# Eight kept weight units instead of six in a streamed mixture-of-experts block, with an earlier reload and folded norms

## The reference, cut to what matters

```python
def first_block(x, ...):                      # 256 tokens, width 1024
    xn = rms_norm(x, norm1_g); h_in = xn @ w_in
    attn = block_attention(q, k, v)           # 8 query heads, 2 key heads
    lru = (h_f + h_b) * gelu(lru_gate)        # two scans, forward and backward
    x = x + concat(rms_norm(attn, g_a), rms_norm(lru, g_l)) @ w_out
    x = x + moe_ffn(rms_norm(x, norm2_g), ...)   # 32 experts, top 4 of them for a token
    return rms_norm(x, final_g)
def moe_ffn(...):                             # for each expert e and its tokens xb
    g = min(xb @ w_gate[e] + b_gate[e], 7); u = clip(xb @ w_up[e] + b_up[e], -7, 7)
    y = ((u + 1) * g * sigmoid(1.702 * g)) @ w_down[e] + b_down[e]
def second_block(x, mem, ...):                # two layers
    h = h + mixer(rmsnorm(h, norm_mix[l]))    # layer 0: index scores choose keys, attention over them,
                                              #   and pooling; layer 1: a convolution module
    h = h + cross_attn(rmsnorm(h, norm_cross[l]), rmsnorm(mem, norm_mem[l]), ...)
    h = h + swiglu(rmsnorm(h, norm_ffn[l]), ...)
```

## Time and profile before

| | before |
|---|---|
| median of 3 runs | 1995.56 us (1995.07 to 1997.11) |
| the profiled execution's own time | 1995.56 us |
| its span, first to last instruction | 1993.8 us |
| TensorE busy | 1968.9 us (99%) |
| VectorE, ScalarE busy | 849.6 us (43%), 421.1 us (21%) |
| moved from and to memory | 565.20 MB, mean 283 GB/s |
| experts, first multiplication to the end of expert 31 | 189.38 to 1123.6 us |

### The profile page before, as it was taken

How to read it: one execution, slowest core, us unless ns; L and a number is a source line. 1 busy time by engine, 2 the same in 40 slices (tenths; PEclk the granted TensorE clock), 3 DMA queues, 4 the chain that set the end, 5 groups by cost and what they waited for, 6 DMA issues and landing times.

```text
span 1993.8 us, 29849 instructions
## 1 busy us (share of the span) xinstructions
PE 1968.9 (99%) x11290; PEld 1281.3 (64%) x11291; DVE 849.6 (43%) x1801; ACT 421.1 (21%) x827; POOL 22.6 (1%) x56
## 2 busy tenths in 40 slices
PE   9999999999999999999999999999999999999999
PEld 7676333333443344333333587889999886989999
DVE  6644212112122112122121367456766697557774
ACT  4442211112212121122122222231100122331100
POOL 0000000000000000000000020000000000000000
PEclk9999999999999999999999999999999999999999
DMA  9258999999999999999999943424445433334430
GB/s 360 98 209 322 420 422 422 418 421 422 422 391 423 420 422 368 423 422 418 421 422 422 422 173 134 187 97 145 167 168 188 190 128 127 138 116 149 170 133 17
DMA packets 81915, 565.20 MB, mean 283 GB/s; under 512 B 10208, under 2 KB 10880, under 8 KB 14240
## 3 DMA queue, kind: packets, MB, share of 16 engines
q1 hardware_dynamic: 80016, 556.92, 69.8%
q0 software_dynamic: 1808, 6.98, 0.9%
HBM read 559.12 MB, written 4.19 MB: 283 GB/s over the span
## 4 chain that ended last, share of the span: by engine, by line
PE 91%; DMA 7%; ACT 1%; issue 0%; DVE 0%; SPq 0%; ACTq 0%; DVEq 0%
PE bank L669 22%; PE bank L1121 17%; PE bank L620 15%; PE bank L1140 9%; DMA ring<-in_stream 7%; PE bank L1061 3%; PE bank L1043 3%; PE bank L720 3%; PE bank L1164 3%; PE bank L828 3%; PE bank L1106 2%; PE bank L1194 1%; PE bank L1052 1%; PE bank L1418 1%; PE bank L692 1%; PE bank L1347 1%
## 5 line engine op out<-in xcount | busy, mean ns | idle before, releaser
L1121 PE MATMUL bank<-ring,sq 128*64 128x512 f32 x1888 | 416.0, 595 | 9.9 <-DMA ring<-in_stream 9.1
L1121 PEld LDWEIGHTS bank<-ring,sq 128*64 128x64 f32 x1888 | 131.9, 137 | 273.1 <-issue 243.6
L1628 ACT ACTIVATE B<-bank 128x256 f32<-128x256 f32 (+1 forms) x206 | 87.6, 455 | 642.9 <-PE bank L669 335.5
L1140 PE MATMUL bank<-ring,sq 128*64 128x512 f32 x896 | 198.5, 596 | 0.0
L620 PE MATMUL bank<-xn,ring 128*128 128x256 f32 x864 | 191.7, 383 | 0.3
L2595 DVE TENSOR_TENSOR xg<-bank,mbias 128x512 f32<-128x512 f32 x32 | 22.1, 691 | 377.3 <-PE bank L1106 332.7
L620 PEld LDWEIGHTS bank<-xn,ring 128*128 128x128 f32 x864 | 164.9, 192 | 25.4 <-issue 3.6
L669 PE MATMUL bank<-B,ring 128*128 128x128 f32 x1280 | 168.0, 275 | 0.0
L669 PEld LDWEIGHTS bank<-B,ring 128*128 128x128 f32 x1280 | 155.2, 192 | 0.0
L1140 PEld LDWEIGHTS bank<-ring,sq 128*64 128x64 f32 x896 | 61.9, 137 | 116.6 <-issue 116.2
L2575 DVE TENSOR_SCALAR B<-B 128x128 f32<-128x128 f32 x66 | 16.0, 284 | 261.9 <-PE bank L1032 261.9
(11 more groups left out here) (443 smaller groups left out, 2277.3 us busy)
## 6 DMA issues: line engine op xcount, KB each, us to landing
ring<-in_stream SPq DMA_DIRECT2D x513, 1024.0 KB, 14.0
B<-in_stream SPq DMA_DIRECT2D x6, 1024.0 KB, 9.0
mem_kv<-ring POOLq DMA_DIRECT2D x2, 1024.0 KB, 7.1
xT<-in_stream SPq DMA_DIRECT2D x2, 1024.0 KB, 16.1
B<-mem_kv POOLq DMA_DIRECT2D x2, 1024.0 KB, 6.6
xT<-in_x SPq DMA_DIRECT2D x4, 256.0 KB, 5.2
ring<-in_stream SPq DMA_DIRECT2D x4, 256.0 KB, 6.0
ring<-in_mem SPq DMA_DIRECT2D x1, 1024.0 KB, 9.8
```

What stands on the lines that cost most here:

```text
L1121: mm = pe.matmul(PS[4 + kind][NARROW * h:NARROW * (h + 1), :], xs[:, k % 4, NARROW * (k // 4):NARROW * (k // 4 + 1)], weights(e, j, kk, h) ...
L1140: mm = pe.matmul(PS[6][NARROW * h:NARROW * (h + 1), :], hT[0][:, f % 4, NARROW * (f // 4):NARROW * (f // 4 + 1)], weights(e, j, kk, h), st ...
L1628: return act.activation(out_, in_, fn, **kw)
```

## The change

Five edits are made together.

- **Kept units.** Eight units are kept instead of six. Unit 4 goes into the first 2048 columns of `tab`, unit 5 into a new tile `short`, which holds what were `std`, `rinv`, `un`, `rb` and `wr`. The second expert that uses kept units is 27 instead of 24. The reloads begin at turn 9 instead of 13, and come ahead of every second turn (9, 11, ... 23) instead of every one.
- **Early slots.** Ring slots 8 and 11 are loaded as soon as `memn` and the second normalised memory are computed and the 16 early units are used, ahead of the kept units. Slots 10 and 9 are loaded after both spills, as before.
- **Tables.** `tab` is ordered anew. Columns 512 to 2047 (`cos2` to `far`) are no longer loaded at the start. ACT loads them (768 KB) when the last scatter's first bank is done; DVE's index rotary waits for it.
- **Folded norms.** DVE adds the two remaining chunks into one (one more addition of 128 x 256), and `stat` has two multiplications fewer. For the LRU group, DVE adds four chunks to two ahead of its maxima of heads 6 and 7, and `group_sum(1)` has two multiplications fewer.
- **The index weights.** The product for `iw` runs with the weights as the stationary operand, 32 columns wide, in four column groups of the array into bank 6. ACT copies the bank, and two multiplications by a table `fold` add the four groups and transpose. They stand behind the first `iqb` unit.

```diff
-KEPT = (3 * E // 16, 3 * E // 4)
-RELOAD = 13 * E // 32
-KEPT_UNITS = (6, 7, 8, 9, 10, 11)
+KEPT = (3 * E // 16, 27 * E // 32)
+RELOAD = 9 * E // 32
+RELOAD_EVERY = 2
+KEPT_UNITS = (4, 5, 6, 7, 8, 9, 10, 11)
...
-        kept = {8: (reg(0, UNIT),), 9: (reg(UNIT, UNIT),), 7: (reg(2 * UNIT, UNIT),),
+        kept = {4: (tab[:, 0:UNIT],), 5: (short[:, :],), 8: (reg(0, UNIT),), 9: (reg(UNIT, UNIT),), 7: (reg(2 * UNIT, UNIT),),
...
+            for u in range(HELD, EARLY + HELD):
+                sp.wait_ge(S["units_done"], u - HELD + 1)
+                load_first(u)
+            sp.wait_ge(S["memn_ready"], 16)
+            load_first(EARLY + HELD)
+            load_first(EARLY + HELD + 3)
+            sp.wait_ge(S["mixed_ready"], 4)
+            for j in (8, 9, 7, 4):
+                keep(KEPT[0], j)
+            sp.wait_ge(S["o_mm"], 8)
+            sp.wait_ge(S["ksum_mm"], 4)
+            for j in (10, 11):
+                keep(KEPT[0], j)
+            sp.wait_ge(S["kv_spilled"], 32)
+            load_first(EARLY + HELD + 2)
+            load_first(EARLY + HELD + 1)
...
                     keep(KEPT[0], 6)
+                    keep(KEPT[0], 5)
...
             for n, j in enumerate(KEPT_UNITS):
                 keep(KEPT[1], j)
-                for s in range(RING):
-                    load_slot(RELOAD + n, s)
+                for i in range(RELOAD_EVERY):
+                    for s in range(RING):
+                        load_slot(RELOAD + RELOAD_EVERY * n + i, s)
...
                 for b in range(2):
-                    for c in range(2):
-                        mm = pe.matmul(PS[stat_bank(n)][:, b:b + 1], sq[:, c, b * P:(b + 1) * P], tb("ones")[:, 0:1],
-                                       start=(c == 0), stop=(c == 1))
+                    mm = pe.matmul(PS[stat_bank(n)][:, b:b + 1], sq[:, 0, b * P:(b + 1) * P], tb("ones")[:, 0:1],
+                                   start=True, stop=True)
...
-            for b in range(2):
-                for k in range(C):
-                    mm = pe.matmul(PS[5][:, T + 16 * b:T + 16 * b + 16], xn[:, k, b * P:(b + 1) * P],
-                                   ring[:, slot_of(u), C * P + 16 * k:C * P + 16 * k + 16],
-                                   start=(k == 0), stop=(k == C - 1))
+            for k in range(C):
+                r = slice(32 * (k % 4), 32 * (k % 4 + 1))
+                mm = pe.matmul(PS[6][r, 0:T], ring[:, slot_of(u), C * P + 32 * k:C * P + 32 * k + 32], xn[:, k, :],
+                               start=(k < 4), stop=(k >= 4), skip_group_check=True)
             mm.then_inc(S["units_done"], 1)
             stationary(AT["iqb"], two(2), xn)
+            pe.wait_ge(S["iwt_ready"], 1)
+            for b in range(2):
+                pe.matmul(PS[5][:, T + 16 * b:T + 16 * b + 16], iwt[:, b * P:(b + 1) * P], tb("fold"),
+                          start=True, stop=True)
...
+            act.wait_ge(S["moe_mm"], 1)
+            lo, hi = TAT["cos2"], TAT["far"] + 2 * T
+            act.dma_start(tab[:, lo:hi], tables[:, lo:hi]).then_inc(S["tables_loaded"], 16)
...
+                    mark(tt(sq[:, 0:2, :], sq[:, 0:2, :], sq[:, 2 * j:2 * j + 2, :], ALU.add))
+                    if j == 3:
+                        settle()
+                        tt(sq[:, 0, :], sq[:, 0, :], sq[:, 1, :], ALU.add).then_inc(S["ssum_ready"], 1)
...
                 if a == 5:
                     dve.wait_ge(S["units_done"], 2)
                     memory(1)
+                    dve.wait_ge(S["osq_ready"], 1)
+                    tt(sq[:, 4:6, :], sq[:, 4:6, :], sq[:, 6:8, :], ALU.add).then_inc(S["osq_ready"], 1)
```

More of the change, by code:

```diff
@@ L106 @@
     NV += _n
-TABLES = [("cos1", T), ("sin1", T), ("cos2", T), ("sin2", T), ("cos3", T), ("sin3", T), ("rot1", P),
-          ("ident", P), ("ones", P), ("heads", P), ("before", P), ("iota", T),
-          ("far", 2 * T), ("rcount", 64)]
+TABLES = [("cos1", T), ("sin1", T), ("cos2", T), ("sin2", T), ("cos3", T), ("sin3", T), ("far", 2 * T),
+          ("rot1", P), ("ident", P), ("ones", P), ("heads", P), ("before", P), ("iota", T), ("rcount", 64), ("fold", 16)]
 TAT = {}
@@ L206, in build @@
         mbias = sb("mbias", [P, E * 16])
-        wr = sb("wr", [P, C, E])
         br = sb("br", [P, E])
@@ L212, in build @@
         pT = sb("pT", [P, 2, 2, T])
-        std = sb("std", [P, 512])
-        rinv = sb("rinv", [P, 512])
+        short = sb("short", [P, UNIT])
+        std, rinv = short[:, 0:512], short[:, 512:1024]
+        un = short[:, 1024:1536].rearrange("p (a t) -> p a t", a=2)
+        rb = short[:, 1536:1792]
+        wr = short[:, 1792:2048].rearrange("p (c e) -> p c e", c=C)
         small = sb("small", [P, 32])
@@ L313, in build @@
         sc = reg(11728, 2, T)
+        iwt = sc[:, 0, :]
         irot = [reg(a, 2, T) for a in (4640, 5152, 3616, 4128)]
@@ L464, in _ @@
                     load_table("ident", "ones", S["vec_loaded"])
[L465 to L468, removed]
+            for dst, src in ((wr, w_router), (br[:, :], b_router), (mbias[:, :], moe_b)):
+                sp.dma_start(dst, src).then_inc(S["router_loaded"], 16)
+            load_table("before", "fold", S["router_loaded"])
             def keep(e, j):
@@ L549, in _ @@
             pool.wait_ge(S["cv_ready"], 4)
-            pool.dma_start(mem_kv[1], ring[:, HELD + 2, :]).then_inc(S["v_spilled"], 16)
+            pool.dma_start(mem_kv[1], ring[:, HELD + 2, :]).then_inc(S["kv_spilled"], 16)
             pool.wait_ge(S["memn_ready"], 16)
@@ L553, in _ @@
             pool.wait_ge(S["kn_ready"], 2)
-            pool.dma_start(mem_kv[0], ring[:, HELD + 1, :]).then_inc(S["k_spilled"], 16)
+            pool.dma_start(mem_kv[0], ring[:, HELD + 1, :]).then_inc(S["kv_spilled"], 16)
             pool.wait_ge(S["res_ready"], 4)
@@ L856, in group_sum @@
             def group_sum(g, bank):
-                pe.wait_ge(S["osq_ready"], 3 - 2 * g)
-                for c in range(4 if g else 2):
-                    mm = pe.matmul(bank[:, 0:T], tb("ones"), sq[:, 4 * g + c, :], start=(c == 0), stop=(c == (3 if g else 1)))
+                pe.wait_ge(S["osq_ready"], 4 - 2 * g)
+                for c in range(2):
+                    mm = pe.matmul(bank[:, 0:T], tb("ones"), sq[:, 4 * g + c, :], start=(c == 0), stop=(c == 1))
                 mm.then_inc(S["ostat_mm"], 1)
@@ L1961, in _ @@
             f(tv[:, 0, 0:T], PS[5][:, 0:T], ACT.Copy).then_inc(S["iq_ready"], 1)
-            f(iw[:, :, :], PS[5][:, T:T + 32].rearrange("p (a b) -> p a b", a=2), ACT.Copy, scale=1.0 / 32)\
-                .then_inc(S["iw_ready"], 1)
+            f(iwt, PS[6][:, 0:T], ACT.Copy).then_inc(S["iwt_ready"], 1)
             for j in range(2):
@@ L1966, in _ @@
                 f(iqr[:, 4 + 2 * j:6 + 2 * j, :], two(2 + j), ACT.Copy).then_inc(S["iq_ready"], 1)
+            f(iw[:, :, :], PS[5][:, T:T + 32].rearrange("p (a b) -> p a b", a=2), ACT.Copy, scale=1.0 / 32)\
+                .then_inc(S["iw_ready"], 1)
             def relu(h):
@@ L2702, in _ @@
             dve.wait_ge(S["un_ready"], UNSCALED[2] + 2)
+            dve.wait_ge(S["tables_loaded"], 16)
             index_rotary(0, index_pair(0), irot[0], index_pair(0))
@@ L3018, in lay_out_stream @@
     one[:, 0:D] = np.concatenate([ik, ik], 1).reshape(C, P, P).transpose(1, 0, 2).reshape(P, D)
-    one[:, D:D + 16 * C] = w[:, 3072:3088].reshape(C, P, 16).transpose(1, 0, 2).reshape(P, 16 * C)
+    one[:, D:D + 32 * C].reshape(P, C, 32)[:, :, 0:16] = w[:, 3072:3088].reshape(C, P, 16).transpose(1, 0, 2)
     s[AT["pool"]][:, 0:4 * P] = a["pool_w_2"][0].transpose(1, 0, 2).reshape(P, 4 * P)
@@ L3111, in lay_out_tables @@
     put("far", np.where(tok[None, None, :] > q, f(FAR), f(0)).reshape(P, 2 * T))
+    put("fold", (i[:, None] % 32 == np.arange(16)[None, :]).astype(f))
     w = 2 ** np.arange(1, 5)[:, None]
```

36 lines of the change are left out of this document (8 added, 28 removed).

## The result

The changed kernel takes 2002.12 us (median of 7 runs, 2000.3 to 2005.15), the kernel before beside it 1995.79 us (7 runs, 1995.07 to 1998.03). The ratio is 1.0032, 95% interval 1.0023 to 1.0041. So it is slower by 6.3 us, where +2.3 was forecast, and its time lies 0.12 us above the upper end of the range. The profiled execution took 2005.15 us, with a span of 2003.3 us. It is thus 3 us above the median. One execution among those reported further down, of the stream's edits alone, took 8288.52 us and is left out of its time and ratio.

A forecast was written before the change was run, and what follows sets the result against it. TensorE, busy 99%, was taken as the bound, with at most 13.2 us lost to late weights. Terms 4.8 + 1.5 - 2.4 - 2.1 + 0.5 = +2.3 us on 1995.56 gave 1997.9 us, range 1990.5 to 2002.

The forecast's parts named there:

- The stream: Expert stage: the new kept units and reloads make weights later, +4.8 us, bounds -0.6 to some 6.3.
- the ledger: Count of the weight ring's lead over TensorE, limit 11.5 us; gave 16.7 us lost against 11.0, slower by 5.7.
- Run B: Narrow experts 13 to 17: 4.6 us lost to late units before, 1.9 forecast with the change.
- run C: Narrow experts 19 to 31: 6.05 us lost to late units before, 10.2 forecast with the change.
- Run A: Narrow experts 0 to 11: 2.6 us lost to late units before, 4.6 forecast with the change.
- 0.9 us of it stays: Of 5 us given at expert 6, only 0.9 remains: lead at expert 7's unit 7 was 10.6, limit 11.5.
- Rival 1: Faster: early reloads cost nothing, expert lateness goes; 1979.9 us at best, 1986.5 with half; 0.15, including what lies between.
- The LRU group's sum: Ahead of the experts (the front): DVE's addition waits for ACT's squares and delays the output projection, +1.5 us, bounds 0 to 1.8.
- The norms: Four fewer TensorE records save 0.4 us in each of norms 2 to 7, -2.4 us; norms 0 and 1 nothing.
- The index weights: Behind the experts: 16 records in column groups 1.0 us, fold 0.4, instead of 3.5; -2.1 us, bounds 0 to -2.3.
- Rival 2: Slower: DVE or tables take over behind the experts, TensorE's 4.5 us lost, 2002.4 us; 0.27, including the stream's upper bounds.
- The tables: Behind the experts: ACT's transfer issue costs +0.5 us; the load is hidden, as DVE needs it 23 us later.

The follow-up runs named there:

- the swaps apart: Changed kernel with POOL's row swaps of the index queries alternating between two semaphores, each waiting for the swap before the last: 1999.0 us, ratio 1.0013.
- the better reloads: Changed kernel, second kept expert 25 instead of 27, reloads ahead of turns 12 to 19: 1994.46 us, 0.9996; also without the LRU addition: 1992.41 us, 0.9984.
- the three profiles at expert 25: Changed kernel with second kept expert 25, reloads at turns 12 to 19: 1994.46 us; without the LRU addition: 1992.41; also with swaps on two semaphores: 1986.51.

## Why the prediction was wrong, point by point

Three terms of the sum failed. In the profiled execution they were off by 0.7 us (stream and tables' issue, 5.3 forecast and 6.0 measured), 3.3 us (front, 1.5 and 4.8) and 3.7 us (index weights, -2.1 and +1.6). The largest is the gain of the index weights, which did not reach the end.

**The stream: the term was too small.** I took 4.8 between 4.0 and 5.7, and the ledger itself had said 5.7. Late units cost 5.6 us more than before (18.8 against 13.2; the rest of the stage's 6.0 is the tables' issue), and 7 us by the ratio when the stream's edits stood alone. Run B came as forecast, 1.6 for 1.9, run C 10.4 for 10.2. The 1.7 us that run C had lost beyond the ledger before did not return. But they were no accident of one run, as I had supposed: six profiles with the stream of before lost 6.0 to 6.6 us there, and what costs them is open. Run A lost 6.8 for 4.6. So the ledger's 5.7 is near the measured 5.6 by luck: what it misses in run C before and in run A after cancels. In run A the step "0.9 us of it stays" failed. The units behind the full ring, unit 7 and unit 8 of expert 7:

```profile
L501 SPq DMA_DIRECT2D ring<-in_stream x2: 328/328/328, 377.2 to 378.9; - x2
...
DMA to landing us min/median/max: 7.4/8.5/9.7
```

Unit 7 lands at 377.23 + 7.36 = 384.6, where it is needed at 383.51 + 12.2 = 395.7: a lead of 11.1, near the limit of 11.5. But unit 8 lands at 378.94 + 9.68 = 388.6, 4.0 us behind it and not 2.5. In this execution the full ring thus cost transfer time on two units. So the lead that goes on from there is 0.4 + 1.5 us less than the 11.5 of the ledger; 4.6 + 1.9 = 6.5, and 6.8 were lost. It is not so behind every full ring. Behind the second wide expert of the kernel before, the loads issued at 787.04 and 788.76 landed 6.92 and 7.65 us later, 2.5 apart. Of the other four profiles with the changed stream three have unit 8 of expert 7 some 2.8 to 3.6 us behind unit 7, and one 2.5. Experts 9 to 11 lost 6.0 to 6.8 us in all four, so the term was too small in each; why the transfers start again as unevenly as this is open.

Rival 1, faster, is refuted. The reload issued at 404.79 landed at 418.39, 2.49 us behind the load ahead of it, and the next load 2.49 us behind the reload: it took its own length from the stream. The Trainium skill (DMA: Bandwidth & Descriptors, Rules for kernel authors) says of issuing early and waiting late that the fixed setup cost overlaps. I had read it as if the whole transfer were free. This trace does not bear that reading out: between full rings the stream stood at 421 to 422 GB/s, and a transfer moved forward displaced another.

**The LRU group's sum: mechanism right, a second effect missing.** The wait was forecast at 1.5 us; the edit alone moved the projection by 1.4. TensorE's wait there grew from 0.73 to 1.50 us, and one of 0.88 us came ahead of it. In the profiles with the addition the experts start at 190.5, 191.8, 191.9, 191.9 and 194.2, in the nine without it at 188.8 to 191.1, medians 191.9 and 189.4: 2.5 us. The rest goes with the granted clock. Four of the five with it show a stretch at 1.2 GHz there, none of the nine without. The fifth (the swaps apart) had the same wait of 1.50 us and kept its clock, and started 1.1 us late. The prediction had priced the wait and nothing behind it. The upper bound of 1.8 was therefore too low.

**The norms: right.** -2.6 us, forecast -2.4.

**The index weights: the product right, its gain lost.** 16 records took 1.07 us (forecast 1.0) and the fold 0.51 (0.4). The bound "0, if DVE's top-k chain should then be the later one" named the right size and the wrong engine. Not DVE's top-k but POOL's swaps, through DVE and ACT, ended later. The room of 23 us that I had seen for the tables said nothing on the swaps. What I had left out of the price is what the faster engine triggers: the ring's loads come earlier and fall onto the swaps. Rival 2 gave 2002.4 by "DVE or the tables take over behind the experts"; that its time is close is luck, as its mechanism is only in part what happened. The norms' gain did reach the end, and in its place the stream and the front cost more.

**The tables: right.** ACT's issue took 0.39 us, landed 9.6 us later, and DVE read the tables at 1160.33 without a wait. **The early slots:** nothing of theirs was seen, as forecast, but no run has them, or the moved tables, alone.

**The sum with what was measured:** stream with the tables' issue +6.0, front +2.5 (median), norms -2.9 with the one ahead of the index weights, index weights between -2.0 (68.8 us in the profile without the addition; 71.0 in that with the better reloads as well) and +1.6 (72.4, with the clock falling behind the waits): +3.6 to +7.2. Measured +6.3.

**What stays open:** why the clock falls in some executions behind the same wait and not in others, why the transfers behind a full ring miss time on one unit in one execution and on two in another, and why the stage of one and the same stream varied by 4.8 us between the three profiles at expert 25.

## What to carry to other kernels

When a kernel streams weights through a ring at full transfer rate, draw up the lead in units (what gives it, what takes it, where the full ring cuts it; here that cost transfer time on one unit or on two), and put a prefetch where the lead is used up just ahead of the next stretch that fills the ring; in a stretch without gaps a prefetch delays the next load by its own length. Where an edit makes TensorE faster, look at which loads it frees earlier and which small dependent transfers on other queues they will meet, and take such a chain apart first. A wait on TensorE in a stretch with several others can cost again in clock: here a wait grown to 1.50 us made the experts 1.1 us late where the clock held, and 2.5 us in the median of five profiles.

## What the runs showed of the hardware that was not expected

- A swap of rows inside on-chip memory, four transfers, took 3.2 us alone and mostly 6 to 8 us with a load of 1 MB issued beside it, though that load itself landed in its usual 5 us.
- Behind a full ring the first load of 1 MB landed 4.2 us behind the one ahead of it and the second 4.0 us behind the first, where the steady distance is 2.49; behind another full ring the second kept to 2.5.
- With the addition the granted clock fell to half for up to 6.7 us behind idle times of 0.8 to 1.5 us, and in one of five profiled executions not at all. 32 records of 256 columns then took 9.21 or 8.18 us in place of 7.14.
- Sixteen records in four column groups took 1.07 us, where 32 full-width ones take 7.14: 3.3 times as fast for each. The Trainium skill (TensorE: Matmul & The Clock Gate, Part 3) has 2.38 for three column tiles; here four gave 3.3.
